# A feed-forward's down projection: who makes the low halves of the weights behind a change of operands

## The reference

```
h = h + y @ w_out
m = rmsnorm(h, gain) @ w_up
h = h + jnp.square(jax.nn.relu(m)) @ w_down      # blocks 1 and 3: 4096 hidden columns
```

## Time and profile before

| | |
|---|---|
| time, median of 3 runs | 4194.0 us (4193.4 to 4198.24) |
| the profiled execution: its time, its span | 4195.38 us, 4193.6 us |
| TensorE matmuls busy | 3710.5 us (88%) |
| VectorE busy | 2719.0 us (65%) |
| ScalarE busy | 1621.1 us (39%) |
| GpSimd busy | 1108.4 us (26%) |

### The profile page before, as it was taken

One profiled execution on the slowest core, in us unless ns is written; L12 is line 12 of the kernel. 1 busy time (PEld: TensorE's weight loads), 2 busy tenths in 40 slices (PEclk: granted clock), 3 DMA queues, 4 the chain that ended last, 5 costly groups with the idle time before them and its releaser, 6 DMA issues. The chain is left out here.

```text
span 4193.6 us, 46898 instructions
## 1 busy us (share of the span) xinstructions
PE 3710.5 (88%) x17662; PEld 3087.3 (74%) x17662; DVE 2719.0 (65%) x2983; ACT 1621.1 (39%) x2178; POOL 1108.4 (26%) x877
## 2 busy tenths in 40 slices
PE   9965999999999986756999999999942979999998
PEld 8953778878878776645788877878832857887886
DVE  3668688776544555456688877544859547887773
ACT  2503344533322234234433343354154454444342
POOL 1110222444222210200232234222220412224451
PEclk9987999999999998978999999999966989999999
DMA  4310245644143322342333344222272442556531
GB/s 138 104 51 10 71 149 163 201 151 160 46 141 115 114 80 56 87 142 80 107 99 115 102 156 146 81 86 86 86 177 65 130 153 71 168 163 201 171 116 66
DMA packets 526854, 482.40 MB, mean 115 GB/s; under 512 B 103364, under 2 KB 415172, under 8 KB 526632
## 3 DMA queue, kind: packets, MB, share of 16 engines
q1 hardware_dynamic: 517272, 445.22, 34.7%
q10 hardware_dynamic: 9360, 34.21, 2.0%
HBM read 321.77 MB, written 157.60 MB: 114 GB/s over the span
## 5 line engine op out<-in xcount | busy, mean ns | idle before, releaser
L955 POOL TENSOR_TENSOR c_wlo<-ff_spare,c_whi 128x512 fp32r<-128x512 f32 x200 | 321.0, 1606 | 572.6 <-ACT c_whi L773 572.1
L1020 PE MATMUL c_acc<-c_hi,c_whi 128*128 128x512 f32 x928 | 362.9, 391 | 8.5 <-issue 8.5
L1022 PE MATMUL c_acc<-c_lo,c_whi 128*128 128x512 f32 x928 | 362.3, 390 | 0.0
L1023 PE MATMUL c_acc<-c_hi,c_wlo 128*128 128x512 f32 x928 | 362.2, 390 | 0.0
L194 POOL TENSOR_TENSOR w_wlo<-w_raw,w_whi 128x1024 fp32r<-128x1024 f32 x60 | 154.8, 2580 | 666.4 <-ACT w_whi L188 666.4
L773 ACT ACTIVATE c_whi<-ff_spare 128x512 fp32r<-128x512 f32 x315 | 198.0, 629 | 341.9 <-PE c_acc L1023 327.8
L1020 PE MATMUL c_acc<-ff_quad,c_whi 128*128 128x512 f32 x696 | 274.9, 395 | 16.8 <-DVE ff_quad L1289 5.5
L1220 DVE TENSOR_TENSOR h<-h,c_acc 128x512 f32<-128x512 f32 x265 | 176.8, 681 | 164.3 <-PE c_acc L1023 164.2
L1023 PE MATMUL c_acc<-ff_quad,c_wlo 128*128 128x512 f32 x696 | 273.5, 393 | 0.0
L1022 PE MATMUL c_acc<-ff_quad,c_whi 128*128 128x512 f32 x696 | 273.3, 393 | 0.0
L194 POOL TENSOR_TENSOR c_wlo<-c_raw,c_whi 128x1024 fp32r<-128x1024 f32 (+1 forms) x53 | 129.2, 2438 | 451.3 <-ACT c_whi L188 451.3
(11 more groups left out here) (743 smaller groups left out, 9931.3 us busy)
## 6 DMA issues: line engine op xcount, KB each, us to landing
c_xs<-hidden SPq DMA_DIRECT2D x67, 1024.0 KB, 8.4
hidden<-c_xs SPq DMA_DIRECT2D x32, 1024.0 KB, 5.4
hidden<-h SPq DMA_DIRECT2D x62, 512.0 KB, 2.8
proj<-c_xs ACTq DMA_DIRECT2D x49, 512.0 KB, 2.6
w_raw<-in_w_in SPq DMA_DIRECT2D x48, 512.0 KB, 4.2
c_raw<-in_w_ff SPq DMA_DIRECT2D x36, 512.0 KB, 5.4
ff_spare<-in_w_ff SPq DMA_DIRECT2D x28, 512.0 KB, 6.7
h<-proj SPq DMA_DIRECT2D x25, 512.0 KB, 5.7
```

The costliest lines, as they stand in the source:

```text
L955: pool.tensor_tensor(ring(s.wlo, n), weight_of(n), ring(s.whi, n).bitcast(F32), ALU.subtract)\
L1020: pe.matmul(to, hi[:, k, :], q_hi[q][:, k, :], start=fresh and k == 0, stop=False, skip_group_check=not fresh)
L1022: pe.matmul(to, hi[:, k, :], q_lo[q][:, k, :], start=False, stop=False, skip_group_check=not fresh)
L1023: mm = pe.matmul(to, lo[:, k, :], q_hi[q][:, k, :], start=False, stop=k == HK - 1, skip_group_check=not fresh)
```

## The change

It redefines `spread`. Before, pairs in `L` and every pair directly behind one of them were excepted; after, pairs in `L` and only the first down pair (`ups`, which is behind the first of `L`) are.

```diff
-    spread = [p > 0 and p != pairs - 1 and p not in L and p - 1 not in L for p in range(pairs)]
+    spread = [p > 0 and p != pairs - 1 and p not in L and p != ups for p in range(pairs)]
     on_dve = [spread[n // 7] and at_product[n] in (DVE_UP if n // 7 < ups else DVE_DOWN) for n in range(N)]
```

## The result

| | before | after |
|---|---|---|
| median of 22 runs each | 4195.09 us (4190.62 to 4204.18) | 4200.84 us (4198.58 to 4204.09) |
| ratio to before | | 1.0014 (95% interval 1.0007 to 1.002) |
| profiled span | 4193.6 us | 4199.9 us |

The change makes the kernel 0.14% slower, clear of the measurement's noise and within the 0.2% that the forecast calls no change. 4198.6 was forecast and 4200.84 measured. Half of the 2.2 between them is the basis: the median of before is 4195.1 over 22 runs, where the three runs that the forecast had gave 4194.0.

The account below looks back on a forecast made before the run. VectorE, slowed by GpSimd, was taken to bound the five touched pairs: 2.40 us added less 1.47 of waits won, 0.92 a pair, 4.6 in all. On the median's 4194.0 that gives 4198.6 us, range 4189 to 4206.

Parts of the forecast that it names:

- the five places: The pairs touched, two in the first feed-forward, one in the second, two in the third; TensorE loses 2.50 us in each.
- Removed and added work: Each touched pair: four low-part subtractions leave GpSimd, and four on VectorE add 0.60 us each, 2.40 in all.
- its walk: Instruction-by-instruction timing of pair 20, first feed-forward: the pair ends 0.92 us later; chance 0.60.
- t2 and t3: VectorE's operand splits of 2048 columns in pair 20, to be 1.09 and 0.50 us shorter without GpSimd's subtractions in the way.
- Who goes first behind t3: GpSimd's waiting low part of (20,3) precedes VectorE's new subtraction, which takes 1.8 us; TensorE stalls 0.89 at (20,1).
- The rival with VectorE first: VectorE's new subtraction precedes GpSimd's behind t3, so (20,1) is not late: 0.32 us a pair, 1.6 in all; chance 0.15.
- The stalls: TensorE idle ahead of (20,1), (20,3), (20,4) and (20,6): about 0.7, 0.1, 0.3 and 1.2 us, in place of two stalls.
- The close call: Pair 21's first mix against GpSimd's (21,0), 0.03 us apart; if GpSimd is first, 1.18 us a pair, 5.9 in all.
- SP's queue: Pair 22's weights, issued about 926.1 instead of 920.11, land by 932, before VectorE reads them near 935: hidden.
- The carry to the end: Products behind each touched pair follow at 2.72 us again, so all five delays reach the end: 4.6 us.
- The relief: Rival: no split or mix meets GpSimd, so 3.98 us of waits go against 2.40 added: 1.58 earlier a pair; chance 0.10.
- The full price: Rival: VectorE's queue pays for all four subtractions and gets nothing back: 2.40 us a pair, 12.0 in all; chance 0.15.

Follow-up runs that it names:

- The short GpSimd subtractions: Kernel before, GpSimd's subtractions in the five pairs cut from 512 columns to 32: 19.04 us a pair; changed kernel with the same cut: 20.57 us.
- The kernels with a part of the change: Kernel before with only P5's, only P2's, or P4's and P7's weight low parts moved to VectorE: 22.15, 22.78, 22.24 us a pair.
- the reordered kernel with all seven: Kernel before with VectorE's mixes and split t6 moved in order, and all seven low parts of the five pairs on VectorE: 19.71 us a pair, ratio 0.9953.

## Why the prediction was right

- **The bound.** VectorE's queue sets the five places, held up by GpSimd. The short GpSimd subtractions show it: they alone bring the pair from 21.54 to 19.04.
- **Removed and added work.** The prediction set 2.40 us a pair of added work against 1.47 of waits won, 0.92 in its walk; 0.90 was measured. The waits that it left to VectorE, 1.10, 0.50 and 0.91, are in the lines above: 1.78 less 0.68, 2.78 less 2.28, and 2.38 less the 1.48 that the two mixes take where they meet next to nothing. The kernels with a part of the change follow the same working.
- **t2 and t3.** They were forecast to take 1.09 and 0.50 us less; they take 2.28 each.
- **Who goes first behind t3.** The prediction had GpSimd, on the strength of the earlier trace rows; the subtraction takes 1.78. Put ahead of t3 it takes 0.68 and the pair 0.58 less. The rival with VectorE first had 0.32 a pair. The kernel with the subtraction ahead of t3 costs the same (21.86 - 21.54); as its order is another one, that is no test of the rival. What rules the rival out is the 1.78.
- **The stalls.** 0.7, 0.1, 0.3 and 1.2 us idle were forecast, and 0.67, 0.11, 0.26 and 1.20 measured.
- **The close call** was the first mix of pair 21 against GpSimd's (21,0), 0.03 us apart by the walk. In all five places and both profiles of the changed kernel VectorE went first, with starts at most 0.03 us apart (917.97 against 917.98 at the first). That the walk fell on this side, and not on 1.18 a pair, is luck: its times are not good to 0.03.
- **SP's queue.** Pair 22's tiles are issued 18.98 us behind the start of (20,0) (923.82 less 904.84) where it was 12.97, and the pairs behind still take 19.04: nothing waits for them, as forecast. A kernel in which the cover is gone was not tried.
- **The carry to the end.** The five places give 4.6 us and the runs 5.8 (2.9 to 8.4). Two profiles of one kernel show the granted clock falling in different places elsewhere; that the rest is such scatter fits them, and the runs' interval is too wide to show it.
- **The rivals.** The relief (-1.58 a pair) would have needed VectorE free of GpSimd. Three subtractions and the neighbours' remain, and even with those of the pair cut short the four cost 1.53. The full price (2.40 a pair) is out by the place's time.

## What to carry to other kernels

Where two engines take turns, count a moved instruction by what it meets in its new place and what it no longer holds up, instruction by instruction; durations alone missed the costs here in both directions (P2's 0.60 cost 1.24, all four's 2.40 cost 0.90). Before work is moved onto a queue that is late, look for what stands in it ahead of the instruction that the bound engine waits for and could stand behind, or fit an idle gap in front: that order was worth 21 us, half of it in pairs where the split of the work never changed, and the split at most 6. Several stalls in a small place are read best from the place's own start-to-start time, which repeats within 0.06 us where the 22 executions of the kernel before spread by 14.

## What the runs showed of the hardware

- Where one of VectorE's splits, mixes or weight subtractions (L1289, L1106, L1293) directly follows another and a weight subtraction of GpSimd (L955) has been in wait for over 0.1 us, GpSimd goes first in 101 of 106 cases over the 14 profiles. The five others are the five places of the reordered kernel with all seven, behind t6, after waits of 1.65 to 1.68 us until the split's end. Behind such splits GpSimd went first after waits of 1.60 to 1.62 us (at the place of the earlier trace rows, once in every profile) and after waits of 2.18 to 2.20 (four times in every profile). What makes the difference stays open.
- A GpSimd subtraction of 32 columns takes 0.25 us alone. It still ends only after the VectorE instruction that it meets, 0.10 us behind it: it takes 2.39 us in the kernel before with the cut, under t4.
- TensorE's granted clock stayed at 1.00 behind the idle times of the five places, 1.25 us at most. Behind those of 1.83 us and more ahead of (15,6) and (16,5), (21,6) and (22,5) in block 2, it mostly fell to about 0.6 for a stretch (0.61 at 822.7 to 827.0 and 0.65 at 842.8 to 847.0 in the kernel before), at some 1.5 us on top of the stall: the product behind takes 4.4 us and not 2.8. Which of them it falls behind varies: pairs 15 and 16 of the third feed-forward took 22.75 and 22.82 us in one profile of the changed kernel, 21.15 and 24.29 in the other.
